# State-space recurrence over chunks of four tokens, two pairs of groups per instruction, in an encoder of two layers

## What is computed

```python
def s5_bidirectional(u, lam_re, lam_im, log_dt, b_re, b_im, c_re, c_im, d_skip):
    y = uf * d_skip
    for direction in range(2):
        a_bar = jnp.exp(lam * dt)
        b_bar = ((a_bar - 1.0) / lam)[..., None] * b_mat
        bu = jnp.einsum('gph,bsgh->bsgp', b_bar, uc)
        _, states = lax.associative_scan(combine, (a_seq, bu), reverse=(direction == 1), axis=1)
        y = y + jnp.real(jnp.einsum('ghp,bsgp->bsgh', c_mat, states))

for layer in range(2):
    proj = rms_norm(x) @ w_in            # q, k, v, u, and two gates of 1024
    a = diff_attention(rotary(q), rotary(k), v)
    s = gelu(s5_bidirectional(u, ...)); s = s * sigmoid(s @ w_glu)
    x = x + (g0 * (a @ w_branch0) + g1 * (s @ w_branch1)) @ w_out
    x = x + (swiglu(x) if layer == 0 else top2_of_8_experts(x))
out = rms_norm(x)
```

## Time and profile before

| | us |
|---|---|
| median of 3 runs | 1583.64 |
| the profiled execution, its own time | 1583.63 |
| its span, first to last instruction | 1581.8 |
| PE / DVE busy | 1483.3 / 1241.0 |
| ACT / POOL busy | 895.2 / 388.1 |

### The profile page before, as it was taken

One profiled execution on the slowest core, in us unless ns is written; L12 is line 12 of the kernel. 1 busy time (PEld: TensorE's weight loads), 2 busy tenths in 40 slices (PEclk: granted clock), 3 DMA queues, 4 the chain that ended last, 5 costly groups with the idle time before them and its releaser, 6 DMA issues.

```text
span 1581.8 us, 21845 instructions
## 1 busy us (share of the span) xinstructions
PE 1483.3 (94%) x7397; PEld 1201.7 (76%) x7397; DVE 1241.0 (78%) x1325; ACT 895.2 (57%) x970; POOL 388.1 (25%) x490
## 2 busy tenths in 40 slices
PE   4989989999998999999899999999999999999996
PEld 3767768788877776677688888888888888888785
DVE  6888967655555789856688988889888898888986
ACT  5632344544455523244476776767767677776774
POOL 6979972910002299900000000000000000000000
PEclk9989999999998999998899999999999999999998
DMA  9421235565544412077399999999999999999980
GB/s 263 161 80 54 80 82 185 182 198 178 191 160 141 134 54 80 28 252 254 129 364 345 348 361 333 351 344 339 362 331 351 345 339 361 331 351 327 355 293 27
DMA packets 269146, 373.48 MB, mean 236 GB/s; under 512 B 12960, under 2 KB 216096, under 8 KB 268960
## 3 DMA queue, kind: packets, MB, share of 16 engines
q1 hardware_dynamic: 265520, 366.47, 68.5%
q0 software_dynamic: 1280, 3.16, 1.0%
q10 hardware_dynamic: 2288, 3.11, 0.6%
HBM read 371.65 MB, written 1.05 MB: 236 GB/s over the span
## 4 chain that ended last, share of the span: by engine, by line
PE 72%; DVE 16%; ACT 5%; issue 4%; POOL 1%; DMA 0%; DVEq 0%; ACTq 0%; POOLq 0%
PE bank L459 69%; DVE lo L1204 4%; ACT hi L864 3%; DVE raw L1303 2%; PE bank L477 1%; DVE raw L1284 1%; PE bank L794 1%; DVE raw L1283 1%; DVE bank L1294 1%; DVE raw L1293 1%; POOL raw L330 1%; DVE at_lo L1640 1%; DVE bank L1295 1%; DVE bank L1296 1%; DVE at_lo L1609 1%
## 5 line engine op out<-in xcount | busy, mean ns | idle before, releaser
L1204 DVE TENSOR_TENSOR lo<-raw,hi 128x2048 fp32r<-128x2048 f32 x347 | 804.5, 2323 | 168.9 <-ACT hi L864 159.6
L864 ACT ACTIVATE hi<-raw 128x2048 fp32r<-128x2048 f32 x347 | 662.9, 1914 | 92.3 <-PE bank L459 91.8
L459 PE MATMUL bank<-hi,at_hi 128*128 128x512 f32 x1280 | 521.2, 407 | 31.8 <-DVE at_lo L1609 7.8
L459 PE MATMUL bank<-hi,at_lo 128*128 128x512 f32 x1280 | 506.4, 396 | 0.0
L459 PE MATMUL bank<-lo,at_hi 128*128 128x512 f32 x1280 | 506.3, 396 | 0.0
L459 PEld LDWEIGHTS bank<-hi,at_hi 128*128 128x128 f32 x1280 | 245.1, 191 | 85.4 <-issue 18.0
L459 PEld LDWEIGHTS bank<-hi,at_lo 128*128 128x128 f32 x1280 | 244.6, 191 | 52.9
L459 PEld LDWEIGHTS bank<-lo,at_hi 128*128 128x128 f32 x1280 | 245.4, 192 | 46.8
L459 PE MATMUL bank<-hi,ht_hi 128*128 128x512 f32 x440 | 172.2, 391 | 4.5 <-DVE ht_lo L1541 3.5
L459 PE MATMUL bank<-lo,ht_hi 128*128 128x512 f32 x440 | 171.3, 389 | 0.0
L459 PE MATMUL bank<-hi,ht_lo 128*128 128x512 f32 x440 | 171.2, 389 | 0.0
(11 more groups left out here) (235 smaller groups left out, 1177.7 us busy)
## 6 DMA issues: line engine op xcount, KB each, us to landing
raw<-in_moe_w_dram SPq DMA_DIRECT2D x528, 512.0 KB, 5.6
raw<-in_ffn_w_dram SPq DMA_DIRECT2D x66, 512.0 KB, 4.3
raw<-in_w_in_dram SPq DMA_DIRECT2D x64, 512.0 KB, 4.7
raw<-in_w_branch_dram SPq DMA_DIRECT2D x16, 512.0 KB, 4.0
raw<-in_w_out_dram SPq DMA_DIRECT2D x16, 512.0 KB, 4.5
raw<-in_w_glu_dram SPq DMA_DIRECT2D x4, 512.0 KB, 4.0
xres<-in_x_dram SPq DMA_DIRECT2D x1, 1024.0 KB, 5.3
areg<-in_norm_mix_dram ACTq DMA_DIRECT2D x2, 512.0 KB, 5.6
```

The source lines that it names most:

```text
L459: return pe.matmul(o, a, b, start=start, stop=stop)
L864: act.activation(hi[:, slot, :], src, ACT.Copy).then_inc(hi_ready, 1)
L1204: tt(lo[:, slot, :], src, hi[:, slot, :].bitcast(f32), SUB).then_inc(lo_ready, 1)
```

## The change

The recurrence goes over chunks of four tokens (64 chunks), and one instruction takes two pairs (a "duo", `m` from 0 to 7), so that a tile still has 512 columns. Powers of A up to four are needed, so the matrices are larger. Tokens are laid on the partitions in another order (partition 64·j + c holds tokens 4c + 2j and 4c + 2j + 1); x and the result are loaded and stored in twice as many DMAs. The small matmuls of the state-space part each use 64 rows of PE's array and 64 (or 16, or 32) of its columns, the two groups of a pair in opposite quadrants. In layer 0 DVE makes the powers of B and the phases' tables and POOL the powers of C; in layer 1 POOL makes all, after the mixer of layer 0. The inner matrix is made by `inner` (192 small matmuls), copied, given its diagonal and moved to other partitions by eight DMAs (`inner_moves`). The transposes of u and b become products with the identity. `ct` of layer 1 moves to the end of layer 0's mixer. After the Gelu, `channels` (16 matmuls) puts the channels back in order.

```diff
-            def s5_in(l, q):
-                if 16 * l + q >= 2:
-                    pe.wait_ge(zs_ready, 16 * l + q - 1)
-                for d in range(2):
-                    for r in range(2):
-                        m = mm(v[:, r, d, :], bbt[r0:r0 + 64, d, r, b, :], rhs, True, True)
+            def s5_in(l, m):
+                for e in range(2):
+                    for d in range(2):
                         for r in range(2):
+                            for g in range(2):
+                                rows = slice(64 * g, 64 * g + 64)
+                                rhs = ut4[rows, 2 * m + e, :] if d == 0 else ut4[rows, 2 * m + e, ::-1]
+                                last = mm(v[rows, r, e, d, :], bbt[rows, 2 * m + e, d, r, :], rhs, True, True)
+            def s5_out(l, m):
+                pe.wait_ge(states_ready, n + 1)
+                if m == 0:
+                    pe.wait_ge(cbm_in, KC_LOADS * (l + 1))
+                for e in range(2):
+                    for d in range(2):
+                        for r in range(2):
+                            for g in range(2):
+                                mm(o[rows, :], cblk[rows, r, q, 4 * d:4 * d + 4, :].rearrange("p i h -> p (i h)"), states,
+                                   d + r == 0, False)
+                    for g in range(2):
+                        last = mm(o[rows, :], cbm[rows, q, :], ut4[rows, q, :], False, True)
+            def inner(l):
+                for b, bank in enumerate((PY[0], PY[1], PV[0], PV[1])):
+                    for i in range(4):
+                        for d, p0, p1 in ((1, 4, 8), (0, 0, 1), (0, 1, 4)):
+                            for r in range(2):
+                                for g in range(2):
+                                    m = mm(bank[64 * g:64 * g + GC, c0:c0 + GC * (p1 - p0)], bbar[rows, r, q, d, :],
+                    m.then_inc(kc_full, 1)
+            def channels(l):
+                pe.wait_ge(gelu_ready, 2 * l + 2)
+                for th in range(TH):
+                    for j in range(2):
+                        for q4 in range(4):
+                            m = mm(o[:, :, j, :], cst[:, C_SEL + 32 * i:C_SEL + 32 * i + 32],
+                    m.then_inc(chan_full, 1)
...
+            def inner_moves(l):
+                act.wait_ge(kc_ready, l + 1)
+                for g in range(2):
+                    for i in range(4):
+                        act.dma_start(cbm[r0:r0 + GC, :, :], kc[64 * g:64 * g + GC, :, GC * (3 - i):GC * (3 - i) + 64]).then_inc(cbm_in, 16)
...
                 phases(l, 0)
+                s5_scan(l, 0)
+                phases(l, 1)
                 for s in range(8):
                     split_static(t + 10 + s)
                     row_max(l, s)
-                    s5_scan(l, 2 * s)
-                    phases(l, 2 * s + 1)
+                    if s < 7:
+                        s5_scan(l, s + 1)
                     softmax_factors(l, s)
-                    s5_scan(l, 2 * s + 1)
                     weights(l, s)
-                    if s < 7:
-                        phases(l, 2 * s + 2)
+                    if s < 6:
+                        phases(l, s + 2)
...
+                phase_products(l, 0)
+                pool.wait_ge(cbm_in, KC_LOADS * (l + 1))
                 for xs in xst:
-                    pool.memset(xs[:, :, 0, 0:1], 0.0)
-                    pool.memset(xs[:, :, 1, P:P + 1], 0.0)
-                phase_products(l, 0)
-                for q in range(PAIRS):
-                    if q + 1 < PAIRS:
-                        phase_products(l, q + 1)
-                    turn_forward(l, q)
+                    pool.memset(xs[:, :, :, 0:1], 0.0)
+                    own.step(pool.memset(xs[:, :, :, 129:130], 0.0))
+                for m in range(DUOS):
+                    if m + 1 < DUOS:
+                        phase_products(l, m + 1)
+                    turn_forward(l, m)
```

More of the change, by code:

```diff
@@ L130, in build @@
         subln = sb("subln", [P, 2, P])
-        small = sb("small", [P, 96])
+        small = sb("small", [P, 128])
         php_last = sb("php_last", [P, 256])
@@ L550, in scores, with states_numbers_t @@
+            def states_numbers_t(l):
+                pe.wait_ge(bc_in, BC_LOADS * (l + 1))
+                for g in range(4):
+                    transposes((l, "ct", g), [craw[g // 2][:, 4 * (g % 2) + i, :, :].rearrange("p a s -> p (a s)") for i in range(4)])
             def scores(l, j, c):
@@ L592, in mixer @@
                 for g in range(2):
-                    transposes((l, "u", g), [u_flat[:, (4 * g + i) * P:(4 * g + i + 1) * P] for i in range(4)])
+                    bank = open_turn((l, "u", g))
+                    for q in range(8):
+                        for g2 in range(2):
+                            for j in range(2):
+                                r0, rows = 64 * g2 + 32 * j, slice(64 * j, 64 * j + 64)
+                                m = mm(bank[r0:r0 + 32, 64 * q:64 * q + 64],
+                                       u_rows[rows, 2 * (8 * g + q) + g2, :, :].rearrange("p t c -> p (t c)"),
+                                       ident[rows, rows], True, True)
+                    m.then_inc(tr_full, 1)
                 proj(t + 4, l, 2, 0, True, False)
@@ L1498, in _ @@
             dve.wait_ge(act_par, 2)
-            a_re, a_im, co_re, co_im, cos, sin, rad2 = (row(PACK + i) for i in range(7))
+            a_re, a_im, co_re, co_im, cos, sin, rad4 = (row(PACK + i) for i in range(7))
             own.step(tt(row(R_t), row(R_sh), row(R_sh), MUL))
@@ L1504, in _ @@
             own.step(tt(a_im, row(R_er), sin, MUL))
-            own.step(tt(rad2, row(R_er), row(R_er), MUL))
+            own.step(tt(rad4, row(R_er), row(R_er), MUL))
+            own.step(tt(rad4, rad4, rad4, MUL))
             own.step(tt(row(R_t), row(R_LR), row(R_LR), MUL))
@@ L1795, in turn_forward, with phase_products @@
-            def turn_forward(l, q):
-                n = 16 * l + q
-                w, xs = wtab[q % 2], xst_flat[q % 2]
+                for k in range(1, 4):
+                    product(tt, own, c_power(k), c_power(k - 1), 32 * l, A_RE, A_IM, pt, True)
+                mark(c_ready)
+            def phase_products(l, m):
+                n = DUOS * l + m
+                if n > 0:
+                    pool.wait_ge(wtab_ready, n)
+                if n >= 2:
+                    pool.wait_ge(zs_used, n - 1)
+                for dst, (r1, r16) in zip([wtab[m % 2][:, 0, :]] + php, ((0, 0), (1, 1), (0, 1), (1, 0))):
+                    last = phase_product(tt, dst, m, r1, r16)
+                last.then_inc(php_ready, 1)
```

534 lines of the change are left out of this document (268 added, 266 removed).

## The result

The changed kernel takes 1574.25 us (median of four runs, 1572.62 to 1575.91) beside 1583.58 (1582.43 to 1583.94) for the one before on the same chip: a ratio of 0.994, 95% interval 0.9925 to 0.9955. It is 9.3 us faster by the medians, where 28.8 were forecast. Its profiled execution took 1573.4 us, 2.0 more than its span of 1571.4; the span before was 1581.8.

A forecast was written before the change was run, and what follows sets the result against it. POOL and DVE were taken to bound the steps. Two stretches at -16.5 us each (-33.0) and +4.2 outside gave -28.8, so 1555 us; its own range 1543 to 1567, the range with rivals 1530 to 1595 (0.8).

The forecast's parts named there:

- What bounds the kernel now: Steps of both mixers: POOL and DVE bound them together, 16.3 us from split to split; PE's real work is less.
- The steps: Each step falls to 11.5 us, bounded by DVE; POOL's work is about 8 us instead of 16, PE's 10.8.
- One product more ... delays the second rotary ... together +2.3: Front of layer 0: u's matmuls and one more DVE product (6 x 0.69 = 4.1 us) together cost 2.3 us.
- In layer 0 DVE has the tables ... so they cost nothing: Layer 0's set-up: DVE's phase tables (about 10 us) and two splits cost nothing; up to 7 us if `inner` were free.
- The set-up: From the end of k's transposes to the first split: 28.5 us, a loss of 19.9 a layer.
- The tail: From the last split of the steps to PE's restart with `proj(t + 16)`: 24.1 us a layer.
- `ct` at the end of layer 0: Layer 1's `ct` comes back at the end of layer 0 as 16 transposes and two waits for ACT's copies: +2.6 us.
- u: Layer 1's front: 128 records of 64 columns take 4.4 us paired instead of 1.0, so +3.4 us.
- Rival A: PE's small matmuls: opposite quadrants don't overlap, 35 us a layer, 70 in all, giving 1625 us; chance 0.17.
- Rival B: Steps of 10.3 us through shorter DVE splits and scans: 15 to 20 us more gain, 1537 us; chance 0.15.
- Rival C: Longer set-up from PE's lower clock or DMAs landing after 7.0 us: 1589 us, within 1575 to 1600; chance 0.12.
- DVE's idle time ahead of the second phases: Sign in the profile after: DVE idle some 10 us there in each layer, with POOL's memset waiting for a DMA.

The follow-up runs named there:

- Experiment 1: Changed kernel, but POOL starts layer 0's C powers only when DVE has made all its B powers: 1570.12 us, ratio 0.9916 to the kernel before.
- experiment 7: Changed kernel, but in layer 0 DVE makes B-bar and the C powers with POOL silent, then POOL makes the four B powers: 1570.79 us.
- 8: Changed kernel, but in layer 0 POOL makes only the tables of phases and DVE all eight products: 1567.32 us, ratio 0.99 to the kernel before.
- experiment 9: Changed kernel, but each of POOL's 18 instructions for layer 0's C powers is cut into two of 128x256: 1573.03 us.
- 5: Changed kernel, but SyncE instead of ScalarE issues the eight transfers of the inner matrix, as soon as it and the B powers are ready: 1569.01 us.
- 6: Changed kernel, but POOL makes the second duo's phase products ahead of its wait for the inner matrix's bands: 1569.47 us.
- experiment 3: Changed kernel, but each layer's last `s5_out` stands behind its projection again, like the other seven: 1559.19 us, ratio 0.9846 to the kernel before.
- experiment 10: Changed kernel without the transposes and copies for layer 1's `ct`, layer 1 using layer 0's numbers: 1571.86 us.

## Why the prediction was wrong, by its own steps

It forecast -28.8 and -9.3 was measured. The sign and what the steps gain were right. Three terms lost 23.4 us, the front of layer 0 (11.4), the set-up (5.5) and the tail (6.5); the steps and layer 1's front gave back some 4. The range of 1530 to 1595 does hold 1574.25, but it was that wide for the rivals, and none of them had the cause: that is luck.

- **"What bounds the kernel now", "The steps": right.** POOL's work is nearly halved, 9.02 us of a step instead of 15.98 (about 8 forecast; its share is 0.79 and not near 0.7), a step takes 11.35 us (11.5), and scan and new wait are as costed. That DVE alone is the bound is not shown: PE is busy for 11.29 of 11.35, where I had 10.8, and the chain goes through it in part.
- **"One product more ... delays the second rotary ... together +2.3": the step that failed**, by 11.4 us. I costed DVE's product instructions at the 0.69 of rows 10. In that row POOL was at small work of its own; in the changed kernel it has 18 instructions of 1.05 at just that time. Beside them DVE's take 1.54. Experiment 1 takes away the neighbour and 12.9 us go; 7, 8 and 9 show how: the two engines take turns instruction by instruction, and the wait follows the length of the other's instruction. I had the same effect before me in the splits, 2.74 beside POOL and 2.2 alone, and used it there only. It was the first rotary that was late, not the second.
- **"In layer 0 DVE has the tables ... so they cost nothing": right as things were** (splits t + 8 and t + 9 at 97.5 and 99.7, inner diagonal behind them at 103.5), because the front was late as well. With the front repaired and POOL's products beside them they cost up to 4 us (experiment 7); I had said up to 7 if `inner` were free.
- **The set-up, mis-sized:** 28.5 forecast, 32.5 and 30.0 measured, 5.5 us in both layers. The issues of the eight transfers took 5.7 and 5.9 instead of 3.6; in layer 0 PE's gaps in `inner` and b are 1.9, and `lam_exp`, which I had left out, stands behind these issues and its table, so that layer 0's first split comes 2.5 us later than layer 1's. Against that the last copy's 0.6 fell out, since the issues start beside it. `inner` and b without their gaps and the landing (2.2) are within 0.8 of what was costed. Experiments 5 and 6 gain 5.2 and 4.8 us by taking single links out.
- **The tail, mis-sized:** 24.1 forecast, 27.4 measured, 6.5 us in both layers. POOL's turn is over 3.9 us after the start of the split (3.5 forecast), `s5_out` takes 2.40 and not 1.4, `channels` 3.64 and not 2.3: these three are 2.7 of the 3.3, and two of them are small matmuls that PE begins after a wait of over 4 us and runs at a granted clock of 0.50. I had the place of the last `s5_out` right in the sum; experiment 3 shows that this place alone costs 7.0 us a layer.
- **`ct` at the end of layer 0:** 2.6 forecast, 3.3 (experiment 10). **u:** 3.4 more forecast; 128 records took 1.99 us, 0.016 each, a quarter of the 0.068 in rows 5. So its four tiles overlap. Without `ct` the piece from the restart to layer 1's k's transposes is 302.1 (experiment 10), 4.2 less than before and not 0.7, which hides 3.5 us of the other errors.

**Rival A fell.** Records in opposite quadrants took 0.031 us, though both write one bank (on different partitions). It would have been 0.068. The Trainium skill (TensorEngine Tiling (Array Packing), Restrictions and Gotchas) forbids different row tiles in one PSUM bank at once; the 268 records in 8.36 us contradict what that rule would make of the time, and the measurement decides. **Rival B fell:** the steps stayed at 11.35; DVE's split stayed at 2.8 beside POOL, and PE's 11.29 busy us would not have fitted into 10.3 either. **Rival C** came closest, 1574.25 being just outside its 1575 to 1600, but for none of its two reasons: in `inner` and b the granted clock was 1.00, and the bands landed in 2.2 us. A longer set-up is 5.5 us of the miss; the largest part, 11.4, is contention, which no rival named. DVE's idle time ahead of the second phases came as said, but in layer 0 it was 13.0 us for `lam_exp`, and only in layer 1 was it for the chain through the DMAs (5.3).

For that the Trainium skill has a rule (SBUF — State Buffer, Who interferes with whom): only the port pair that DVE and GpSimd share causes contention, and it is an exclusive lock. The trace agrees in the main: 1.47 us from start to start is 0.60 of DVE and 0.87 of waiting, most of one of POOL's 1.05, and with POOL's instruction halved DVE's is 0.43 shorter (experiment 9). By that rule the two products would have been 12 x (0.60 + 1.05) = 19.8 us instead of 7.2, an estimate; 18.7 were measured, and the front was about 12 us later.

## What to carry to other kernels

Read the cost of a DVE instruction with two operands in SBUF together with what POOL does at that moment: beside POOL add up to one whole instruction of POOL's to each (0.87 of 1.05 here), so keep POOL's instructions short or away from the chain that sets the end. When work is moved ahead of a long operation, cost the wait that comes with its new place and not only the work. A chain through five engines is as long as the queue behind each of its links: put issues and table loads where nothing on the chain stands behind them.

## What the hardware showed that I had not expected

- The turn-taking added about 0.8 us to a DVE instruction of any length, so short ones suffer most: 64 elements went from 0.2 to 1.0 us, 512 from 0.60 to 1.47, and the split of 2048 from 2.2 to about 3.0. Instructions that read PSUM (rotary, 0.74) kept their time.
- Opposite quadrants of PE overlap if they alternate in the stream: 0.031 us a record, and 0.048 if eight of one stand in a row.
- The eight transfers within SBUF cost their queue 0.71 us of issue each on ACT's and 0.84 on SyncE's, where rows 10 had 0.33 and 0.62 for other loads.
- After 4.24 us of waiting PE's next 40 records of small matmuls took 2.40 instead of 1.38, at a granted clock of 0.50, so a wait cost more than its length.
- The level of PE's clock at a restart was worth 2.2 us in layer 0 and 3.2 us in layer 1, with the same instructions behind it.
